# Moving the index score products of a two-block transformer kernel from the end of each projection tile to three places inside it

## Chip, cores and metric

The kernel runs on one core of a Trainium2 chip. The metric is device time in microseconds (us) of one execution; the median of three runs of the kernel before is 3087.84 us (3087.29 to 3089.44).

## What is computed

The reference is a stack of two kinds of transformer block over 512 tokens of width 1024. The first kind (latent attention, Fourier mixing and windowed attention, then a feed-forward and a gated embedding) is run twice, the second kind once. The change lies in the second kind, which begins with one wide projection `h @ w_in` and feeds, among others, a sparse attention. The keys of this attention are picked by an "index branch":

```python
logits = einsum('bqhd,bsd->bqhs', q_idx, k_idx) * IDX_DIM ** -0.5          # 8 heads of 64
score  = einsum('bqh,bqhs->bqs', w_idx * IDX_HEADS ** -0.5, relu(logits))
score  = where(admissible, score, -inf)
_, sel = top_k(score, 128)                                                 # per query
```

## The kernel before, in words

Weights arrive as a stream of units of 1 MB (128 partitions by 2048 columns, that is 16 blocks of 128x128). Every unit is split into a high part (`w_hi`, ScalarE, L923) and a low part (`w_lo`, VectorE, L1318), and every block of a projection is three TensorE matmuls of 512 columns: high by high, low by high, high by low (`mac`, L504 to L506). SyncE starts the load of a unit when VectorE has split the one that was in the same buffer before (`lo_ready`); there are two buffers of each kind.

The stage "z2" is the wide projection of the second block: 23 tiles (n = 0 to 22) of 8 blocks (j = 0 to 7), so 24 matmuls in a tile and two tiles in a unit. Results go round PSUM banks 0 to 3. `run` (L515) writes TensorE's order: for each tile it waits for a free bank, goes through the blocks, signals `tile_done`, and calls `after(n)`. Tiles 4 to 7 are the index queries `qi`, tile 8 the index keys `ki`, tile 9 holds the head weights.

Between these tiles the index branch is worked off: 32 score products, t = 0 to 31, one for each of 4 query blocks b = t // 8 and 8 heads hh = t % 8. A product (L823) is a float32 matmul with 64 rows of contraction and (b+1)*128 columns; its rows are partitions 0 to 63 for an even head and 64 to 127 for an odd one. It goes to one of two score banks, t % 2. `idx_items(n)` gives three products to each tile from n = 11 (two to n = 21). ScalarE takes the relu into `sq[:, t % 2]` (L1219), VectorE multiplies by the head's weight and adds to `score` (`add_idx`, L1723 and L1726). The rings are two deep:

```python
                    if t >= 2:
                        pe.wait_ge(idx_relu, t - 1)       # L820, TensorE: relu of product t-2
```

```python
                    if t >= 2:
                        act.wait_ge(idx_added, t - 1)     # L1217, ScalarE: add of product t-2
```

All three products of tile n stand behind its last block (`after_z2`, L816). ScalarE's and VectorE's orders are written by hand as well: each calls `evac_z2(n)` for both tiles of a unit, and then its part of the split of the unit two further on. Within `evac_z2(n)` the tile's own result comes first and the three relus or adds of that tile behind it. On ScalarE tile 14 also has four casts of `ua_hi` (L971) and a table load for the Gelu; on VectorE tiles 14 to 17 have the pooling windows (`pool`, L1704 to L1711), and tiles 18 to 22 end with one round of `take_top8` (L1740, L1741).

The stages behind z2 are "lru" (12 single blocks), the merges "bm2" and "am", and the sparse attention "dsa", in which two more blocks of a projection stand behind each step.

Of the kernel before, what the change touches and what calls it, by code (L numbers as in the profile page):

```python
# [11 lines left out]
ACT = mybir.ActivationFunctionType  # L12
AX_X = mybir.AxisListType.X

P = 128
S = 512
# [209 lines left out]
def block_kernel(nc, stream, xT, pT, memT, vec1, cst, pos, out):  # L226
    with ExitStack() as ctx:
# [16 lines left out]
        sq = sb("sq", 108, [2, S])  # L244
# [109 lines left out]
        SCORES, TURNED, VALUES = bank[4:6], bank[6], bank[7]  # L354
# [63 lines left out]
        idx_done = sem("idx_done")  # L418
        idx_relu = sem("idx_relu")
# [37 lines left out]
        def idx_items(n):  # L457
            return range(min(3 * max(n - IDX_FROM, 0), IDX_ITEMS), min(3 * max(n - IDX_FROM + 1, 0), IDX_ITEMS))
        assert idx_items(22).stop == IDX_ITEMS


        NORMS = {
# [32 lines left out]
        def _(pe):  # L495
# [15 lines left out]
                    pe.wait_ge(tile_free, c.at("T", st, n - 3))  # L511
                return bank[t % 4]

            def run(c, st, operand, first=0, last=None, width=S, after=None, together=False):


                tiles = TILES[st]
                u0 = c.base[st]["U"]
                ends = {}
                for n, t in enumerate(tiles):  # L520
                    for j, b in enumerate(t):
                        ends[b // BLK] = (n, j)
                seen = -1 if first == 0 else tiles[first - 1][-1] // BLK
                if together:
                    pe.wait_ge(lo_ready, c.at("U", st, 1))
                    seen, first = 0, 2
                    two = [free_bank(c, st, n)[:, 0:width] for n in range(2)]
                    for j in range(KD):
                        for n in range(2):
                            xh, xl, need = operand(n, j)  # L530
                            if need is not None:
                                pe.wait_ge(need[0], need[1])
                            mm = mac(two[n], u0 % 2, tiles[n][j], P, xh, xl, j == 0, j == KD - 1)
                            if j == KD - 1:
                                mm.then_inc(tile_done, 1)
                    if after is not None:
                        after(1)
                for n in range(first, len(tiles) if last is None else last):
                    t = tiles[n]
                    ps = free_bank(c, st, n)[:, 0:width]  # L540
                    for j, b in enumerate(t):
                        u = b // BLK
                        if u > seen:
                            pe.wait_ge(lo_ready, c.at("U", st, u + 1))
                            seen = u
                        xh, xl, need = operand(n, j)
                        if need is not None:
                            pe.wait_ge(need[0], need[1])
                        mm = mac(ps, (u0 + u) % 2, b % BLK, P, xh, xl, j == 0, j == len(t) - 1)
                        if j == len(t) - 1:  # L550
                            mm.then_inc(tile_done, 1)
                        elif ends[u] == (n, j):
                            mm.then_inc(part_done, 1)
                    if after is not None:
                        after(n)

# [253 lines left out]
            def after_z2(n):  # L810
                if n == 10:
                    pe.wait_ge(act_took, c.at("A", "z2", 9))
                    for t in range(ST):
                        mm = nc.tensor.transpose(TURNED[:, t * P:(t + 1) * P], vwT[:, t * P:(t + 1) * P], ident)
                    mm.then_inc(vw_turned, 1)
                for t in idx_items(n):  # L816
                    if t == 0:
                        pe.wait_ge(tile_free, c.at("T", "z2", 9))
                    if t >= 2:
                        pe.wait_ge(idx_relu, t - 1)  # L820
                    b, hh = t // 8, t % 8
                    r = slice(64 * (hh % 2), 64 * (hh % 2) + 64)
                    nc.tensor.matmul(SCORES[t % 2][:, 0:(b + 1) * P], qi[r, hh // 2, b * P:(b + 1) * P], ki[r, 0:(b + 1) * P],  # L823
                                     start=True, stop=True).then_inc(idx_done, 1)
            run(c, "z2", lambda n, j: (h_hi[:, j, :], h_lo[:, j, :], (res_split, c.at("R", "norm1", j + 1)) if n == 0 else None),
                together=True, after=after_z2)

            def lru_operand(n, j):
                if n < 4:
# [43 lines left out]
        for table, stages in ((RR1, STAGES1), (RR2, STAGES2)):  # L873
            n = 0
# [32 lines left out]
        def _(act):  # L907
# [287 lines left out]
            link(nc.scalar.activation(lruc[:, 2, 0:4], lruc[:, 1, 0:4], ACT.Ln, bias=1.0))  # L1195
            nc.scalar.activation(lruc[:, 3, 0:4], ap4, ACT.Relu, scale=-1.0).then_inc(softplus_ready, 1)

            def evac_z2(n):
                if n < 4:
                    take_hi(c, "z2", n, n, lx[:, n, :])  # L1200
                elif n < 8:
                    take_hi(c, "z2", n, n, qi[:, n - 4, :])
                elif n == 9:
                    take_hi(c, "z2", n, 8, vwT[:, :])
                elif 14 <= n < 18:
                    if n == 14:
                        for j in range(4):
                            split_hi(c, "z2", j, ua_hi[:, j, :], ua[:, j, :], (res_ready, result_value(c, "z2", j)))
                    take_hi(c, "z2", n, n - 5, lg[:, n - 14, :], ACT.Gelu_apprx_tanh)
                elif n == 19:  # L1210
                    for j in range(4):
                        r = c.base["z2"]["R"] + 4 + j
                        split_hi(c, "z2", 4 + j, pool_hi[:, j, :], res[:, r % 4, :], (res_ready, result_value(c, "z2", 4 + j)))
                for t in idx_items(n):
                    act.wait_ge(idx_done, t + 1)
                    if t >= 2:
                        act.wait_ge(idx_added, t - 1)  # L1217
                    w = (t // 8 + 1) * P
                    nc.scalar.activation(sq[:, t % 2, 0:w], SCORES[t % 2][:, 0:w], ACT.Relu).then_inc(idx_relu, 1)  # L1219
            stage_loop(c, "z2", evac_z2)  # L1220

            def evac_lru(n):
# [75 lines left out]
        def _(dve):  # L1298
# [416 lines left out]
            def add_idx(t):  # L1715

                b, hh = t // 8, t % 8
                w = (b + 1) * P
                dve.wait_ge(idx_relu, t + 1)
                if t == 0:  # L1720
                    dve.wait_ge(res_ready, result_value(c, "z2", 3))
                if hh == 0:
                    ins = nc.vector.tensor_scalar(score[:, b, 0:w], sq[:, t % 2, 0:w], wsc[:, b, hh:hh + 1], None, ALU.mult)  # L1723
                else:
                    dve.wait_ge(idx_added, t)
                    ins = nc.vector.scalar_tensor_tensor(out=score[:, b, 0:w], in0=sq[:, t % 2, 0:w], scalar=wsc[:, b, hh:hh + 1],  # L1726
                                                         in1=score[:, b, 0:w], op0=ALU.mult, op1=ALU.add)
                ins.then_inc(idx_added, 1)
# [16 lines left out]
            A_Z2 = {n: n for n in range(8)} | {9: 8} | {n: n - 5 for n in range(14, 18)}  # L1745

            def evac_z2(n):
                if n in A_Z2:
                    dve.wait_ge(act_took, c.at("A", "z2", A_Z2[n] + 1))
                    pass_on(c, "z2", n)  # L1750
                    if 4 <= n < 8:
                        conv(n - 4)
                    elif n >= 14:
                        if n == 14:
                            dve.wait_ge(tile_free, c.at("T", "z2", 14))
                        pool(n - 14)
                elif 10 <= n < 14:
                    if n == 10:
                        dve.wait_ge(pad_ready, 1)
                    copy_out(c, "z2", n, 0, pz[:, n - 10, PADW:PADW + S], lambda ps: ps[:, :], wait_act=False)  # L1760
                    if n == 10:
                        dve.wait_ge(vw_turned, 1)
                        link(nc.vector.tensor_copy(vw[:, :, :], TURNED[:, :].rearrange("p (t d) -> p t d", t=ST)))

                        link(nc.vector.tensor_scalar(wsc[:, :, :], vw[:, :, HD:HD + 8], 8 ** -0.5, None, ALU.mult))
                else:
                    dst = {8: ki, 22: kk}.get(n)
                    copy_out(c, "z2", n, 0, qd[:, n - 18, :] if dst is None else dst[:, :], lambda ps: ps[:, :], wait_act=False)
                for t in idx_items(n):
                    add_idx(t)  # L1770
                if n >= 18:
                    if n == 18:
                        dve.wait_ge(idx_added, 16)
                        hide(1)
                    take_top8(rounds[n - 18])
# [379 lines left out]
```

## Time and profile before

| what | value |
| --- | --- |
| runs | 3087.84 us median (3087.29 to 3089.44) |
| profiled execution | span of 3080.3 us from first to last instruction; the page gives no other time of it |
| TensorE matmuls busy | 2884.8 us, 94% of the span |
| VectorE busy | 1541.7 us, 50% |
| ScalarE busy | 1072.0 us, 35% |
| GpSimd busy | 458.7 us, 15% |
| granted TensorE clock | 0.969 of full speed over the span |
| the products, L823 | 64 matmuls, between 2126.7 and 2204.6 us |

Times in the rows are microseconds from the start of the span. The median of the runs is 7.5 us above the span. A matmul's own duration contains the passage through the array; the time that it costs is read from one start to the next. A row of the timeline may merge matmuls of one line ("x4").

### The profile page before, as it was taken

The numbers are of one execution on the slowest core, as the hardware profiler recorded it, in microseconds if no ns is written. First come the engines' busy times: TensorE is split into PE (matmuls) and PEld (weight loads), VectorE is DVE, ScalarE is ACT, GpSimd is POOL, SyncE is SP. The second block draws the span as 40 slices with busy tenths as digits, with TensorE's granted clock in tenths as the row PEclk, the third lists the DMA queues.
The fourth block names the chain that finished last, engine by engine and source line by source line (L and its number), as shares of the span: only waits on it lengthen the run. The fifth ranks groups of instructions, "written<-read, shape, count | busy, mean of one in ns | idle before, by whom it ended". The sixth has DMA issues, their size and how long they took to land. (4 is left out here: it accounts for less than half of the span.)

```text
span 3080.3 us, 34797 instructions
## 1 busy us (share of the span) xinstructions
PE 2884.8 (94%) x12356; PEld 2227.7 (72%) x12356; DVE 1541.7 (50%) x2229; ACT 1072.0 (35%) x1631; POOL 458.7 (15%) x283
## 2 busy tenths in 40 slices
PE   6998999899999899899989999989999998899997
PEld 4875567688887688546768888767676676578886
DVE  4356684534324534768444342454578735553333
ACT  4234433332323433443233222342533333432221
POOL 1010011311102301001131111230011113121101
PEclk9999999999999899999999999999998899999999
DMA  3221012222232222101222223222222122122232
GB/s 125 96 83 55 15 55 83 69 96 95 95 110 91 68 96 86 65 1 56 82 82 82 95 95 109 86 69 91 82 97 81 42 71 80 41 82 95 95 109 83
DMA packets 37047, 245.80 MB, mean 80 GB/s; under 512 B 4144, under 2 KB 5168, under 8 KB 7984
## 3 DMA queue, kind: packets, MB, share of 16 engines
q1 hardware_dynamic: 33600, 239.09, 22.8%
q10 hardware_dynamic: 3312, 4.93, 0.5%
q8 instruction: 82, 1.34, 0.2%
q14 instruction: 53, 0.43, 0.0%
HBM read 241.91 MB, written 2.10 MB: 79 GB/s over the span
## 5 line engine op out<-in xcount | busy, mean ns | idle before, releaser
L504 PE MATMUL bank<-h_hi,w_hi 128*128 128x512 f32 x2152 | 865.3, 402 | 53.8 <-DVE h_lo L1401 40.8
L505 PE MATMUL bank<-h_lo,w_hi 128*128 128x512 f32 x2152 | 846.1, 393 | 0.0
L506 PE MATMUL bank<-h_hi,w_lo 128*128 128x512 f32 x2152 | 845.9, 393 | 0.0
L1318 DVE TENSOR_TENSOR w_lo<-raw,w_hi 128x2048 fp32r<-128x2048 f32 x225 | 519.4, 2309 | 559.4 <-ACT w_hi L923 384.1
L504 PEld LDWEIGHTS bank<-h_hi,w_hi 128*128 128x128 f32 x2152 | 409.4, 190 | 161.7 <-issue 35.7
L505 PEld LDWEIGHTS bank<-h_lo,w_hi 128*128 128x128 f32 x2152 | 409.6, 190 | 86.8 <-issue 4.7
L506 PEld LDWEIGHTS bank<-h_hi,w_lo 128*128 128x128 f32 x2152 | 408.9, 190 | 87.1
L923 ACT ACTIVATE w_hi<-raw 128x2048 fp32r<-128x2048 f32 x137 | 261.9, 1911 | 313.5 <-PE bank L506 303.5
L504 PE MATMUL bank<-a_hi,w_hi 128*128 128x512 f32 x528 | 205.4, 389 | 0.0
L505 PE MATMUL bank<-a_lo,w_hi 128*128 128x512 f32 x528 | 205.4, 389 | 0.0
L506 PE MATMUL bank<-a_hi,w_lo 128*128 128x512 f32 x528 | 205.4, 389 | 0.0
L1873 POOL TENSOR_TENSOR a_lo<-res,a_hi 128x512 f32 x66 | 85.8, 1300 | 632.8 <-ACT a_hi L1061 632.8
L1508 DVE TENSOR_TENSOR res<-bank,rstd 128x512 f32<-128x512 f32 x66 | 45.6, 691 | 235.2 <-PE bank L506 235.2
L1891 POOL TENSOR_TENSOR w_hi<-raw,cst_sb 128x2048 fp32r<-128x2048 f32 x20 | 72.0, 3602 | 531.5 <-PE bank L506 490.3
L1061 ACT ACTIVATE a_hi<-res 128x512 f32 x66 | 41.7, 632 | 301.4 <-DVE res L1511 301.4
L1018 ACT ACTIVATE pT<-bank 128x512 f32<-128x512 f32 (+3 forms) x168 | 82.8, 493 | 150.7 <-PE bank L641 147.8
L1065 ACT ACTIVATE w_hi<-raw 128x2048 fp32r<-128x2048 f32 x66 | 125.5, 1902 | 0.0
L1897 POOL TENSOR_TENSOR x<-x,sg 128x512 f32<-128x512 f32 x60 | 108.9, 1820 | 95.1 <-DVE sg L1366 62.7
L504 PEld LDWEIGHTS bank<-a_hi,w_hi 128*128 128x128 f32 x528 | 99.1, 188 | 20.7
L506 PEld LDWEIGHTS bank<-a_hi,w_lo 128*128 128x128 f32 x528 | 99.1, 188 | 20.6
L505 PEld LDWEIGHTS bank<-a_lo,w_hi 128*128 128x128 f32 x528 | 99.1, 188 | 20.4
L932 ACT ACTIVATE sq<-bank 128x512 f32<-128x512 f32 x64 | 38.3, 598 | 211.6 <-PE bank L506 211.2
(351 smaller groups left out, 4030.5 us busy)
## 6 DMA issues: line engine op xcount, KB each, us to landing
raw<-in_stream SPq DMA_DIRECT2D x226, 1024.0 KB, 4.9
x<-in_xT SPq DMA_DIRECT2D x2, 1024.0 KB, 12.0
out_T<-x ACTq DMA_DIRECT2D x8, 256.0 KB, 2.1
p_f<-in_pT ACTq DMA_DIRECT2D x2, 512.0 KB, 3.7
memf<-in_memT ACTq DMA_DIRECT2D x1, 1024.0 KB, 5.6
cst_sb<-in_cst ACTq DMA_DIRECT2D x1, 411.5 KB, 6.2
pos_i<-in_pos ACTq DMA_DIRECT2D x1, 258.0 KB, 8.8
vec<-in_vec ACTq DMA_DIRECT2D x2, 26.0 KB, 1.7
```

The lines of the kernel that those rows point to most:

```text
L504: nc.tensor.matmul(ps, wh, xh, start=start, stop=False)
L505: nc.tensor.matmul(ps, wh, xl, start=False, stop=False)
L506: return nc.tensor.matmul(ps, wl, xh, start=False, stop=stop)
L923: nc.scalar.activation(w_hi[v % 2][:, :], raw[v % 2][:, :], ACT.Copy).then_inc(hi_ready, 1)
L1018: nc.scalar.activation(a["pT"][h % 2][:, 0:n, b * P:(b + 1) * P], TURNED[:, 0:n * P].rearrange("p (t q) -> p t q", t=n), ACT.Copy).then_in ...
L1061: nc.scalar.activation(a_hi[:, bass.ds(i * 2 + p, 1), :].rearrange("p a s -> p (a s)"), res[:, p, :], ACT.Copy).then_inc(res_hi, 1)
L1065: nc.scalar.activation(w_hi[v][:, :], raw[v][:, :], ACT.Copy).then_inc(hi_ready, 1)
L1318: nc.vector.tensor_tensor(w_lo[s][:, :], raw[s][:, :], w_hi[s][:, :].bitcast(F32), ALU.subtract).then_inc(lo_ready, 1)
L1508: nc.vector.tensor_tensor(res[:, p, :], bank[(t0 + 2 * p + 1) % 4][:, :], rstd[:, 0, :], ALU.mult).then_inc(tile_free, 1)
L1873: nc.gpsimd.tensor_tensor(a_lo[:, bass.ds(i * 2 + p, 1), :].rearrange("p a s -> p (a s)"), res[:, p, :], a_hi[:, bass.ds(i * 2 + p, 1), :] ...
L1891: nc.gpsimd.tensor_tensor(w_hi[v % 2][:, :], raw[v % 2][:, :], ones[:, 0:1].to_broadcast([P, UC]), ALU.mult).then_inc(pool_hi_ready, 1)
L1897: nc.gpsimd.tensor_tensor(x[:, m, :], x[:, m, :], sg[:, m % 2, :], ALU.add).then_inc(x_ready, 1)
```

## The change

The products of tile n are no longer all behind its last block: the first stands behind block j = 1, the second behind j = 4, the third behind j = 7. `run` gets a hook `within(n, j)` that is called behind each block. ScalarE and VectorE take the first two relus or adds of a tile ahead of the tile's own result, and the third behind it, as before. The waits themselves are unchanged, and so are the transposes behind tile 10.

```diff
+        IDX_AFTER = (1, 4, 7)
@@ run
-            def run(c, st, operand, first=0, last=None, width=S, after=None, together=False):
+            def run(c, st, operand, first=0, last=None, width=S, after=None, together=False, within=None):
@@
                         elif ends[u] == (n, j):
                             mm.then_inc(part_done, 1)
+                        if within is not None:
+                            within(n, j)
@@ TensorE, z2
-                for t in idx_items(n):
+
+            def logits_idx(n, j):
+
+                items = idx_items(n)
+                for t in items[IDX_AFTER.index(j):][:1] if j in IDX_AFTER else ():
                     if t == 0:
                         pe.wait_ge(tile_free, c.at("T", "z2", 9))
                     if t >= 2:
@@
-                together=True, after=after_z2)
+                together=True, after=after_z2, within=logits_idx)
@@ ScalarE
+            def relu_idx(t):
+                act.wait_ge(idx_done, t + 1)
+                if t >= 2:
+                    act.wait_ge(idx_added, t - 1)
+                w = (t // 8 + 1) * P
+                nc.scalar.activation(sq[:, t % 2, 0:w], SCORES[t % 2][:, 0:w], ACT.Relu).then_inc(idx_relu, 1)
+
             def evac_z2(n):
+                for t in idx_items(n)[0:2]:
+                    relu_idx(t)
...
-                for t in idx_items(n):
-                    act.wait_ge(idx_done, t + 1)
-                    if t >= 2:
-                        act.wait_ge(idx_added, t - 1)
-                    w = (t // 8 + 1) * P
-                    nc.scalar.activation(sq[:, t % 2, 0:w], SCORES[t % 2][:, 0:w], ACT.Relu).then_inc(idx_relu, 1)
+                for t in idx_items(n)[2:]:
+                    relu_idx(t)
@@ VectorE
             def evac_z2(n):
+                for t in idx_items(n)[0:2]:
+                    add_idx(t)
...
-                for t in idx_items(n):
+                for t in idx_items(n)[2:]:
                     add_idx(t)
```

## Rows read from the trace of the kernel before

**Rows 1.** Busy time, clock and DMA share in the stretch with the products.
```profile
core 0: us, PE busy (x) PEld busy (x) DVE busy (x) ACT busy (x) POOL busy (x), PEclk, DMA share, GB/s
2126.00:2206.00 80.00, 75.22 (x315) 52.14 (x314) 47.65 (x72) 30.06 (x51) 12.21 (x8) 1.00 0.20 66
```

**Rows 2.** TensorE's waits in the same stage: engine, line, releaser, us, times, longest.
```profile
PE bank L823 <- ACT sq L1219: 4.8, 10, 0.7
```

**Rows 3.** TensorE's timeline, undisturbed blocks of tile 7, 18 matmuls apart.
```profile
start us, us, engine line op out<-in xcount [idle before <-releaser]
2100.02 0.39 PE L506 MATMUL bank<-h_hi,w_lo 128*128 128x512 f32 x1
...
2104.10 0.39 PE L506 MATMUL bank<-h_hi,w_lo 128*128 128x512 f32 x1
```

**Rows 4.** TensorE's timeline, first matmul of tile 11.
```profile
2121.00 0.48 PE L504 MATMUL bank<-h_hi,w_hi 128*128 128x512 f32 x1
```

**Rows 5.** TensorE's timeline, end of tile 20, its products, first matmul of tile 21.
```profile
2194.50 0.39 PE L506 MATMUL bank<-h_hi,w_lo 128*128 128x512 f32 x1
2194.82 1.13 PE L823 MATMUL bank<-ki,qi 64*128 64x512 f32 x4
2196.63 1.12 PE L823 MATMUL bank<-ki,qi 64*128 64x512 f32 x2 [0.68 <-ACT sq L1219]
2197.68 0.50 PE L504 MATMUL bank<-h_hi,w_hi 128*128 128x512 f32 x1
```

**Rows 6.** TensorE's timeline, the two products of tile 21, start of tile 22.
```profile
2203.35 1.13 PE L823 MATMUL bank<-ki,qi 64*128 64x512 f32 x4
2204.41 0.50 PE L504 MATMUL bank<-h_hi,w_hi 128*128 128x512 f32 x1
2204.74 0.39 PE L505 MATMUL bank<-h_lo,w_hi 128*128 128x512 f32 x1
```

**Rows 7.** TensorE's timeline, third product of tiles 12, 14 and 17, next block.
```profile
2134.47 0.48 PE L823 MATMUL bank<-ki,qi 64*128 64x128 f32 x2 [0.36 <-ACT sq L1219]
2134.89 0.50 PE L504 MATMUL bank<-h_hi,w_hi 128*128 128x512 f32 x1
...
2148.89 0.70 PE L823 MATMUL bank<-ki,qi 64*128 64x256 f32 x2 [0.47 <-ACT sq L1219]
2149.51 0.50 PE L504 MATMUL bank<-h_hi,w_hi 128*128 128x512 f32 x1
...
2171.80 0.91 PE L823 MATMUL bank<-ki,qi 64*128 64x384 f32 x2 [0.57 <-ACT sq L1219]
2172.64 0.50 PE L504 MATMUL bank<-h_hi,w_hi 128*128 128x512 f32 x1
```

**Rows 8.** TensorE's timeline, windowed attention: one 64-row product between two blocks.
```profile
348.96 0.40 PE L506 MATMUL bank<-h_hi,w_lo 128*128 128x512 f32 x1
349.29 0.91 PE L631 MATMUL bank<-kdup,qc 64*128 64x384 f32 x2
350.13 0.50 PE L504 MATMUL bank<-h_hi,w_hi 128*128 128x512 f32 x1
350.47 0.40 PE L505 MATMUL bank<-h_lo,w_hi 128*128 128x512 f32 x1
```

**Rows 9.** TensorE's timeline, latent attention: one 96-row product between two blocks.
```profile
248.72 0.39 PE L506 MATMUL bank<-h_hi,w_lo 128*128 128x512 f32 x1
248.95 1.02 PE L631 MATMUL bank<-k_a,q_a 96*128 96x512 f32 x2
249.41 0.80 PE L504 MATMUL bank<-h_hi,w_hi 128*128 128x512 f32 x1
250.04 0.40 PE L505 MATMUL bank<-h_lo,w_hi 128*128 128x512 f32 x1
```

**Rows 10.** ScalarE's timeline, tile 14: the casts and the table load.
```profile
2144.24 2.18 ACT L971 ACTIVATE ua_hi<-ua 128x512 fp32r<-128x512 f32 x4
2146.44 1.28 ACT L932 ACT_TABLE_LOAD   x1
```

**Rows 11.** VectorE in stage bm2; TensorE at the start of the sparse attention.
```profile
2239.97 0.69 DVE L1422 TENSOR_TENSOR merged<-bank,sg 128x512 f32<-128x512 f32 x1 [11.69 <-ACT sg L932]
...
2366.30 0.79 PE L631 MATMUL bank<-kk,qd 64*128 64x128 f32 x2 [5.77 <-DVE rstd L1425]
```

## The prediction

> **What bounds the kernel now.** I read the stretch with the products first. TensorE is busy for 75.22 of 80 us at the full clock, VectorE for 47.65, ScalarE for 30.06, and the DMA engines for a fifth [rows 1]. So TensorE sets the pace here, and only what TensorE issues or waits for can change the time. Next its waits: all that is named is ten waits of a product for a relu, 4.8 us together [rows 2]. They are what the change can remove: the third product of a tile needs the bank of the first, and so the relu of a product issued just before it. Tile 21 has two products and no wait, which makes ten waits in the eleven tiles.
>
> Then the price of all 32 products. Undisturbed, 18 steps from one matmul to the next take 2104.10 - 2100.02 = 4.08 us, 0.2267 us each [rows 3], so a tile of 24 matmuls takes 5.44 us. From the first matmul of tile 11 (2121.00) [rows 4] to the first of tile 22 (2204.41) [rows 6] there are 83.41 us. Eleven tiles take 59.85 of them; the products with their waits cost **23.56 us**.
>
> **What makes them cheap is the pair.** The first two products of a tile stand together, and one uses partitions 0 to 63, the other 64 to 127. Four matmuls (two products) of 512 columns show 1.13 us, and two matmuls (one product) show 1.12 [rows 5]. From the start of a pair to the next block it is 2204.41 - 2203.35 = 1.06 us [rows 6]; from the start of a single product it is 2197.68 - 2196.63 = 1.05 us [rows 5]. The second product of a pair is free. The change takes every pair apart.
>
> **The change part by part.** (1) It adds no instruction, moves no DMA, and does not change what has to be computed. (2) It puts each of the 32 products by itself between two blocks. What one costs there: the step from the last block to the product is 2194.82 - 2194.50 = 0.32 us [rows 5], the product to the next block is 0.42, 0.62, 0.84 us at 128, 256, 384 columns [rows 7] and 1.05 at 512, and the first step within the block after is 2204.74 - 2204.41 = 0.33 [rows 6]. Without the product the first and the last of these would be two ordinary steps, 0.454 us. So it costs 0.62, 0.82, 1.04 and 1.25 us at the four widths, 3.73 for one of each. The single products of rows 5 and 7 stand behind a wait, which might flatter them. The windowed attention has the very thing, one 64-row product of 384 columns between two blocks with no wait: 350.47 - 348.96 = 1.51 us, less 0.454 is 1.06 [rows 8], against my 1.04. With eight products of each width the sum is 8 x 3.73 = 29.8 us.
>
> (3) The steps behind a break are a little slow. Tile 21 takes 2203.35 - 2197.68 = 5.67 us from its first matmul to its pair [rows 5, 6]; less 0.33 and 0.32 that leaves 5.02 for 22 steps, 0.2282 each, 0.033 us more per tile than at 0.2267. The 23.56 us hold one such tail per tile, and three breaks per tile may make up to three. If every tail stays whole that is 32 x 0.033 = 1.1 us, if they cost nothing more 0; I take 0.8, since the nine steps between two breaks hold most of a tail. The products then cost 29.8 + 0.8 = 30.6 us.
>
> (4) The ten waits go; they are inside the 23.56. The difference is 30.6 - 23.56 = **+7.0 us**. As a cross-check by tile: tile 21 now pays 2 x 1.25 = 2.50 us where it paid 1.06 + 0.32 + 0.33 - 0.454 = 1.26, so +1.24. Tile 20 paid the 0.32, then 1.81 from pair to third product and 1.05 onward, and the 0.33: 3.06 in all; it now pays 3.75, +0.69, though a wait is gone. In the wait of about 0.7 us TensorE already covered most of what a separate product costs.
>
> (5) Moved on ScalarE: two relus of each tile now stand ahead of its eviction and wait for products behind blocks 1 and 4. Behind them on this engine is only the eviction of the same tile, not ready before block 7. Tile 14 is the tight place: `ua_hi` casts (2.18 us) and table load (1.28 us) [rows 10] now begin after the relu behind block 4, some 5.4 us into a tile that takes 5.44 + 3 x 0.82 = 7.9 us. Eviction and third relu follow, done about 9.9 us in. Product 13, which needs this relu, stands behind block 4 of tile 15, at 7.9 + 15 x 0.2267 + 0.82 = 12.1 us. Margin 2 us, so I cost it at nothing; if that cover were gone, TensorE would wait.
>
> (6) Moved on VectorE: two adds go ahead of the tile's own work, where it now waits for a relu in the middle of the tile. Behind that wait is only the copy of the same tile; the bank it frees is needed four tiles later. The low split of a unit still follows the odd tile at once, and the SyncE load that it releases is for a buffer used two units on; with the queues a fifth busy [rows 1] nothing waits for it. The pooling of tiles 14 to 17 delays the third add, and with it a relu one product later, but every relu has at least three blocks and a product (over 2.6 us) more than before. Costed at nothing.
>
> The sum in microseconds is the same against the span (3080.3) or the median of the runs (3087.84), which stands 7.5 us above it: 3087.84 + 7.0 = **3094.8 us**. A difference of 0.2% (6.2 us) is about what a measurement of this kernel can tell from no change, so my forecast stands just over that line.
>
> **Bounds.** What one product costs between blocks has a far lower end: the latent attention has a 96-row product of 512 columns between blocks, and 250.04 - 248.72 = 1.32 us less 0.454 is 0.87 [rows 9], 0.38 under my 1.25. With 96 rows no pair is possible, and the step into it is 0.23 and not 0.32. Were the 32 products as smooth, they would cost 30.6 - 32 x 0.38 = 18.4 us, and the change would give -5.2 us. Rows 8 have the very shape, so I take 1.25. The upper end is rows 8's extra 0.02 on each, +0.6 us.
>
> **The rivals.** A, faster: a product's weights are loaded beneath the block before it, so that a product is all streaming, as in rows 9; it decides if the extra per product is under (23.56 - 18.4) / 32 = 0.16 us of the 0.38. Then 3087.84 - 5.2 - 1 (the tails gone too) = 3081.7 us. For it: a weight load of an ordinary block is hidden in this way at every step of 0.2267 us. Against it: rows 8.
>
> The Trainium skill, "TensorE: Matmul & The Clock Gate", section "Step-by-step: what each phase is for", says that a weight load is pulled ahead of running matmuls when the row groups do not conflict or it goes to the background buffer. By the second half of that rule A would hold, with 3081.7 us; rows 8 and 5 speak against it, since a 64-row product costs more than its stream there.
>
> B, slower still: a new wait takes the place of the old one, in tiles 14 to 18, where ScalarE's or VectorE's moved work makes a relu late and a product stands in the middle of an open tile. At 1 us in each of four or five tiles that is +4.5, so 3099 us. For it: in the kernel before, relus there wait for adds behind the pooling. Against it: the margins of (5) and (6).
>
> C, no change: a later stage gives the time back. The sparse attention starts with TensorE waiting 5.77 us for VectorE [rows 11]. If VectorE got there by its own backlog, a slower z2 would shrink that wait, to 3087.84 + 7.0 - 5.8 = 3089.0 us. Against it: in bm2 VectorE idles 11.69 us for a ScalarE result [rows 11], which follows TensorE's tiles, so the backlog does not reach back to z2.
>
> **How the numbers follow.** My forecast has 0.78, with its own range 3092 to 3097. Rows 8's price and full tails would give +7.9, no tails and the low roundings +6.1: I put 0.50 above the line of 6.2 us and 0.28 under. A has 0.06 (0.04 faster, 0.02 within), B 0.08 (slower), C 0.08 (within). Faster 0.04, within 0.38, slower 0.58. The range takes in C and most of B: 3089 to 3099.
>
> **What would show it.** Right: no row of L823 with x4 and no pair starting within 0.1 us; no wait of L823 for `sq`; a product to the next block at 0.42, 0.62, 0.84 and 1.05 us; first matmul of tile 11 to first of tile 22 about 83.4 + 7.0 = 90.4 us; the stages behind z2 shifted by that and no more. Wrong: a product at under 0.9 us in all at 512 columns (A); waits of L823 in tiles 14 to 18 (B); a stretch of z2 that is 7 us longer with a span that is not (C).

## The result, and the profile after

The changed kernel takes 3093.66 us, the median of 13 runs (3088.89 to 3095.1), against 3087.84 us for 13 runs of the kernel before. The ratio is 1.0018 with a 95% interval of 1.001 to 1.0026: slower by 3 to 8 us. Forecast were 3094.8 us and a range of 3089 to 3099. The two profiled executions differ by 6.8 us in span (3080.3 and 3087.1).

The busy times of the stage come first (columns as in rows 1).

```profile
core 0: us, PE busy (x) PEld busy (x) DVE busy (x) ACT busy (x) POOL busy (x), PEclk, DMA share, GB/s
2126.00:2206.00 80.00, 80.00 (x289) 49.33 (x287) 45.23 (x68) 28.95 (x47) 11.01 (x8) 1.00 0.19 66
```

TensorE now shows busy for all of the 80 us, against 75.22 in [rows 1]. Yet it starts 289 matmuls in them, and 315 before. The busy share rose and the work done fell. The 4.8 us that were idle before are the ten waits of [rows 2]. All other time shows as busy in both kernels, whether blocks follow at their 0.23 us or a product stands between them, because the row of a matmul (0.39 us for one of a block) lasts past the start of the next.

The view of TensorE's waits over 2117 to 2222 us has no row for a product any more, where [rows 2] had ten. The view of the product's line (L830 in the changed kernel) says what its two queues waited for.

```profile
L830 PEld LDWEIGHTS bank<-ki,qi x64: 182/184/186, 2122.5 to 2208.6; 64*128 64x128 f32 x64
L830 PE MATMUL bank<-ki,qi x64: 272/481/693, 2122.5 to 2209.1; 64*128 64x128 f32 x16, 64*128 64x256 f32 x16, 64*128 64x384 f32 x16, 64*128 64x512 f32 x16
its engine sat idle before it (us, times) until:
  issue: 11.5, 32
```

Each of the 32 products now has its own gap ahead of its weight load (PEld, the queue of weight loads), 0.36 us on average, and none waits for the relu. The same 64 matmuls have the same durations as before. Only their company has changed.

TensorE's timeline, the first and second products of tile 20 and the blocks round them:

```profile
2195.92 1.12 PE L830 MATMUL bank<-ki,qi 64*128 64x512 f32 x2
2196.97 0.50 PE L505 MATMUL bank<-h_hi,w_hi 128*128 128x512 f32 x1
2197.30 0.39 PE L506 MATMUL bank<-h_lo,w_hi 128*128 128x512 f32 x1
...
2198.92 0.39 PE L507 MATMUL bank<-h_hi,w_lo 128*128 128x512 f32 x1
2199.24 1.12 PE L830 MATMUL bank<-ki,qi 64*128 64x512 f32 x2
2200.29 0.50 PE L505 MATMUL bank<-h_hi,w_hi 128*128 128x512 f32 x1
2200.62 0.39 PE L506 MATMUL bank<-h_lo,w_hi 128*128 128x512 f32 x1
```

The steps are 0.32, 1.05 and 0.33 us, those of [rows 5, 6]; at the other widths 0.41, 0.63 and 0.84 us stand in the place of the 1.05, as in [rows 7]. In the kernel before, the row of the pair had "x4" and 1.13 us for twice the work.

The stretch from the first matmul of tile 11 to the first of tile 22:

```profile
2120.98 0.48 PE L505 MATMUL bank<-h_hi,w_hi 128*128 128x512 f32 x1
...
2211.76 0.39 PE L505 MATMUL bank<-h_hi,w_hi 128*128 128x512 f32 x1
```

It is 90.78 us, where it was 83.41 [rows 4, 6]: +7.37 us. Less the 59.85 us of the eleven tiles without products, the 32 products cost 30.9 us instead of 23.6. Behind z2 two rows answer to [rows 11]; the first is VectorE's, the second TensorE's.

```profile
2247.15 0.69 DVE L1434 TENSOR_TENSOR merged<-bank,sg 128x512 f32<-128x512 f32 x1 [11.68 <-ACT sg L939]
...
2373.45 0.79 PE L634 MATMUL bank<-kk,qd 64*128 64x128 f32 x2 [5.76 <-DVE rstd L1437]
```

They start 7.18 and 7.15 us later, after the same idle times (11.69 and 5.77 before). The stages between pass the delay on unchanged, up to 0.2 us. From the end of the stretch to the end of the span it is 875.9 us before and 875.3 after, so in these two executions at most 0.6 us are given back.

### The profile page after: what moved, and what is told of

It reads as the page before. It is cut to its first block and busy times, and to the rows that moved or that the text cites. A ratio compares the mean times of both kernels' runs of the same rounds, so it can differ in the third digit from the quotient of the medians.

```text
span 3087.1 us, 34795 instructions
## 1 busy us (share of the span) xinstructions
PE 2897.7 (94%) x12356; PEld 2229.8 (72%) x12356; DVE 1540.4 (50%) x2229; ACT 1073.2 (35%) x1631; POOL 457.3 (15%) x283
```

## The experiments

In each trace I read the stretch from tile 11 to tile 22, because the profiled executions already differ by up to 6 us ahead of it (tile 11 starts between 2120.98 and 2126.91), where the kernels are the same. Each interval of a ratio is about 5 to 8 us wide, so the runs give the sign and rough size, and the stretch tells kernels apart. Times are against runs of the kernel before on the same chip.

**The new order on ScalarE and VectorE alone.** From the changed kernel:

```diff
-        IDX_AFTER = (1, 4, 7)
+        IDX_AFTER = (7,)
@@ logits_idx
-                for t in items[IDX_AFTER.index(j):][:1] if j in IDX_AFTER else ():
+                for t in items if j == 7 else ():
```

> The new order on ScalarE and VectorE alone; TensorE's three products stand behind the last block of a tile, as before. 'Stretch' is the time from the first matmul of tile 11 to the first of tile 22: 83.4 us before, 90.8 after. Theory (the pairs taken apart on TensorE are the whole cost): stretch 83 to 84 us, ten waits of L830 for sq of about 4.8 us in total, time as before within 0.5 us. Rival (the new order on the other two engines costs): stretch over 86 us, with waits of L830 longer than 1 us.

Measured: 3087.11 us against 3088.62, ratio 0.9994 (0.9985 to 1.0004). Its stretch goes from 2125.57 to 2209.24, 83.67 us. The waits of TensorE in the stage, and tile 15's products in its timeline:

```profile
PE bank L830 <- ACT sq L1210: 4.8, 10, 0.7
```

```profile
2159.77 0.70 PE L830 MATMUL bank<-ki,qi 64*128 64x256 f32 x4
2160.94 0.70 PE L830 MATMUL bank<-ki,qi 64*128 64x256 f32 x2 [0.47 <-ACT sq L1210]
2161.57 0.50 PE L505 MATMUL bank<-h_hi,w_hi 128*128 128x512 f32 x1
```

The ten waits of [rows 2] are back with the pairs, and the loss is gone. The order of the relus and adds costs nothing that can be seen (0.26 us of stretch). The cost of the change is on TensorE. The expectation of a time within 0.5 us can't be checked: the runs give 1.5 us less, with an interval of -4.6 to +1.2.

**Pairs kept, waits gone.** The pair behind block 1, the third product behind block 5; all relus and adds of a tile ahead of its own result:

```diff
-        IDX_AFTER = (1, 4, 7)
+        IDX_AFTER = {1: slice(0, 2), 5: slice(2, 3)}
@@ logits_idx
-                for t in items[IDX_AFTER.index(j):][:1] if j in IDX_AFTER else ():
+                for t in items[IDX_AFTER[j]] if j in IDX_AFTER else ():
@@ evac_z2 of ScalarE and VectorE
-                for t in idx_items(n)[0:2]:
+                for t in idx_items(n):
...
-                for t in idx_items(n)[2:]:
```

> The first two products of a tile stand together behind block 1, the third behind block 5: pairs kept, waits gone. Theory: 21 breaks in place of 32, priced by their widest product at 0.62, 0.82, 1.04 and 1.25 us, 19.7 us and 0.5 for tails: stretch 80.1 us, 3.3 less than before and 10.7 less than after. Rival (what costs is that a product stands inside an open tile, whatever it is): per tile two breaks inside a tile in place of one outside, stretch over 84 us.

Measured: 3083.2 us against 3088.62, ratio 0.9983 (0.9974 to 0.9992). Stretch 80.52 us, 0.4 more than expected. TensorE's timeline, the third product of tile 20 and the pair of tile 21:

```profile
2196.54 1.12 PE L830 MATMUL bank<-ki,qi 64*128 64x512 f32 x2
2197.59 0.50 PE L505 MATMUL bank<-h_hi,w_hi 128*128 128x512 f32 x1
...
2200.55 1.13 PE L830 MATMUL bank<-ki,qi 64*128 64x512 f32 x4
2201.61 0.50 PE L505 MATMUL bank<-h_hi,w_hi 128*128 128x512 f32 x1
```

1.05 us for one product, 1.06 for two, both inside an open tile and without a wait. So it does not matter that a tile is open. With the pairs left whole, being rid of the 4.8 us of waits is worth 2.9 us net, since the third product still pays its own break.

**All products in pairs.** Sixteen places, 5.5 blocks apart:

```diff
-        IDX_AFTER = (1, 4, 7)
+        IDX_AT = [89 + 11 * p // 2 for p in range(IDX_ITEMS // 2)]
+
+        def idx_pairs(n, js=range(8)):
+            return [t for p, g in enumerate(IDX_AT) if g // 8 == n and g % 8 in js for t in (2 * p, 2 * p + 1)]
...
```

The lines left out make all three engines take the products of a tile from `idx_pairs`. ScalarE and VectorE take a pair ahead of the tile's own result, or behind it if the pair stands behind block 7.

> All 32 products in 16 pairs, one every 5.5 blocks. Theory: four breaks of each width, 4 x 3.73 = 14.9 us and 0.4 to 0.5 for tails: stretch 75.2 us, time 8.2 us less than before (-0.27%). Rival (the price belongs to the product, not to the break): 32 products cost as in after, stretch about 90 us, or, with a relu not ready at the next pair, waits of L83x for sq and a stretch over 78.

Measured: 3079.42 us against 3088.62, ratio 0.9969 (0.9957 to 0.9982). Stretch 75.58 us, and no wait for `sq`. Two pairs from TensorE's timeline, at 256 and 384 columns:

```profile
2159.53 0.70 PE L832 MATMUL bank<-ki,qi 64*128 64x256 f32 x4
2160.16 0.50 PE L508 MATMUL bank<-h_hi,w_hi 128*128 128x512 f32 x1
...
2164.48 0.92 PE L832 MATMUL bank<-ki,qi 64*128 64x384 f32 x4
2165.32 0.50 PE L508 MATMUL bank<-h_hi,w_hi 128*128 128x512 f32 x1
```

0.63 and 0.84 us, what a single product of the width costs. The 32 products cost 75.58 - 59.85 = 15.7 us, half of the 30.9 of the changed kernel. The price goes by the break, and the second product in it is free.

**Single products over all 128 rows.** A product sums two heads here, so the logits of the index branch are other ones.

```diff
-                    r = slice(64 * (hh % 2), 64 * (hh % 2) + 64)
+                    r = slice(0, P)
```

> As after, but each product is taken over all 128 partitions, so that it sums two heads: the logits of the index branch are those of two heads added, and the rest is unchanged. Theory (0.38 us of every single product is the change between 64 and 128 rows of the array, not the stream): 0.24, 0.44, 0.66 and 0.87 us a product as in rows 9, 17.7 us in all: stretch 77.6 to 78.6 us, about 5 us less than before and 12 less than after. Rival (the extra belongs to a float32 matmul among the rounded ones, or to the smaller weight load): stretch as in after, 90.8 us.

Measured: 3082.87 us against 3088.62, ratio 0.9983 (0.9973 to 0.9992). Stretch 2121.25 to 2199.59, 78.34 us. TensorE's timeline, one product of 512 columns:

```profile
2188.30 0.39 PE L507 MATMUL bank<-h_hi,w_lo 128*128 128x512 f32 x1
2188.53 1.02 PE L830 MATMUL bank<-ki,qi 128*128 128x512 f32 x2
2188.98 0.80 PE L505 MATMUL bank<-h_hi,w_hi 128*128 128x512 f32 x1
2189.62 0.40 PE L506 MATMUL bank<-h_lo,w_hi 128*128 128x512 f32 x1
```

The weight loads of this product, and those of the 64-row product that starts at 2199.24 in the changed kernel:

```profile
2188.30 0.41 PEld L830 LDWEIGHTS bank<-ki,qi 128*128 128x128 f32 x2
```

```profile
2199.23 0.29 PEld L830 LDWEIGHTS bank<-ki,qi 64*128 64x128 f32 x2 [0.35 <-issue]
```

The 128-row load begins together with the last matmul of the block before, 0.23 us ahead of its product. The 64-row load begins 0.31 us after the last matmul of its block (2198.92), 0.01 us ahead of its product. So 128-row weights are loaded beneath the block, and 64-row weights are not.

From block to block 2189.62 - 2188.30 = 1.32 us, the same as in [rows 9], and 0.38 less than 0.32 + 1.05 + 0.33 for 64 rows. Type, width, place and number are those of the changed kernel; only the rows differ, and with them the size of the weight load. So it is not the float32 type that costs. That it is not the small load by itself either is shown by the groups of four below, which have the same 64 small loads. And 96 rows are as smooth as 128 [rows 9]. In this stretch the step between 64-row and 128-row matmuls costs 90.78 - 78.34 = 12.4 us, or 0.39 us for each product's way in and out.

The Trainium skill, "TensorE: Matmul & The Clock Gate", section "The mechanism", finds weight loads overlapping running matmuls only where the row groups differ. A 64-row product between 128-row blocks shares rows with both, and by that rule its load is exposed, as here. But a 128-row product shares them too, and its load is hidden (2188.30 above), so the rule as it stands does not tell the two apart and does not give the 0.39 us. What in the engine holds the 64-row load back no run here shows.

**Groups of four.** Eight places, ten blocks apart, and four score banks:

```diff
-        IDX_AFTER = (1, 4, 7)
+        IDX_AT = [97 + 10 * q for q in range(IDX_ITEMS // 4)]
+        SCORES4 = (bank[4], bank[5], bank[6], bank[7])
@@ logits_idx
-                    if t >= 2:
-                        pe.wait_ge(idx_relu, t - 1)
+                    if t >= 4:
+                        pe.wait_ge(idx_relu, t - 3)
...
```

The lines left out write product t to `SCORES4[t % 4]`, let ScalarE read it there, and let all three engines take the products of a tile in groups of four.

> The 32 products in eight groups of four, one every ten blocks from block 1 of tile 12, over four score banks: two pairs share one way in and one way out. Theory: a break has 0.38 us for its way in and out and the stream 0.24, 0.44, 0.66, 0.87 for each pair; eight breaks are 8 x 0.38 + 4 x 2.21 = 11.9 us and 0.2 for tails: stretch 72.0 us, 3.6 less than with sixteen pairs. Rival 1 (the price is per pair, not per break): stretch 75.6 as with sixteen pairs. Rival 2 (ScalarE or VectorE fall behind with four relus and adds at once): waits of TensorE for sq of over 1 us in tiles 14 to 18.

Measured: 3077.28 us against 3088.23, ratio 0.9969 (0.9957 to 0.998). Stretch 2126.23 to 2198.23, 72.00 us. TensorE's timeline, one group of 512 columns:

```profile
2190.42 0.39 PE L511 MATMUL bank<-h_hi,w_lo 128*128 128x512 f32 x1
2190.74 1.99 PE L833 MATMUL bank<-ki,qi 64*128 64x512 f32 x8
2192.66 0.50 PE L509 MATMUL bank<-h_hi,w_hi 128*128 128x512 f32 x1
2192.99 0.40 PE L510 MATMUL bank<-h_lo,w_hi 128*128 128x512 f32 x1
```

1.92 us from the group to the next block, against 1.06 for one pair: the second pair adds 0.86 us, its stream alone. The way in and out is paid once per group. Four products take two streams, not four and not one: the even and the odd head of a pair, in different halves of the rows, run together, and the next pair follows. No run puts two products of the same half side by side, so that the halves are the reason is a reading. ScalarE and VectorE keep up, with no wait of TensorE for `sq`. By the stretch this is the best of the kernels tried, 11.4 us shorter than before; the runs can't separate it from the sixteen pairs.

**The changed kernel again.**

> The changed kernel once more, beside runs of the kernel before of the same hour: the stretch should be 90.8 us again and the time 7 us more than before (+0.23%) if all that the stretch adds reaches the end; rival: about 5.6 us (+0.18%), so that 1 to 2 us are given back behind it.

Measured: 3093.23 us against 3088.23, ratio 1.0018 (1.0009 to 1.0027), and a stretch of 90.79 us. The ratio is the same as the first time, and its interval (2.8 to 8.3 us) holds both 7 and 5.6 us, so the runs did not tell the two apart. The trace speaks against the rival: from the end of the stretch to the end of the span it is 875.1 us, against 875.9 before, so 0.8 us are given back and not 1 to 2.

## Why the prediction was right

By its own steps:

- **What bounds.** TensorE's order alone sets the stage. The order of the other two engines on its own moved the stretch by 0.26 us.
- **The pair is free.** Shown: 1.05 us for one and 1.06 for two, in the same kernel; the same at 256 and 384 columns; half the price when all products are in pairs.
- **Step 2, the price of a single product.** 29.8 us for 32, from steps that came out the same to 0.01 us. Averaged over the eight products of each width, the prices in the changed kernel are 0.62, 0.83, 1.04 and 1.26 us, 30.0 in all. The row of another stage with the very shape [rows 8] was a better guide than the smooth one [rows 9], as chosen.
- **Step 3, the tails.** I took 0.8 us, and 30.9 - 30.0 = 0.9 is left for them. The 0.2 us of step 2 and the 0.1 here are most of the difference between +7.0 and the +7.37 of the stretch.
- **Step 4, the waits.** They went, all ten, and were worth less than what took their place.
- **Step 5, ScalarE in tile 14.** Shown below. Tile 14 starts at 2143.33, and the third relu ends at 2153.18, 9.85 us in (9.9 predicted). Product 13, which needs it, starts at 2155.82, 2.6 us later. The margin held.

```profile
2148.82 2.18 ACT L978 ACTIVATE ua_hi<-ua 128x512 fp32r<-128x512 f32 x4
2151.02 1.28 ACT L939 ACT_TABLE_LOAD   x1
2152.31 0.60 ACT L939 ACTIVATE lg<-bank 128x512 f32<-128x512 f32 x1
2152.80 0.38 ACT L1210 ACTIVATE sq<-bank 128x256 f32<-128x256 f32 x1
```

- **Rival A** (a product is all streaming) is what the 128-row experiment shows: its weights are loaded beneath the block, and the stretch is 78.34 us, 5.1 less than before, where the rival's price said 5.2. It takes 128 rows, which this change does not have.
- **Rival B** (a new wait) did not come: no wait of a product in any tile.
- **Rival C** (given back by the sparse attention's wait) did not come either: that wait is 5.76 us, 7.15 of the 7.37 us arrive there, and 6.8 us are left at the end of the span.

The mechanism stands by the stretch. In the time as run, +7.0 was forecast and the ratio gives +5.6 us. That is under the line of 6.2 us (0.2%) above which the prediction put a chance of 0.50, while the stretch, at +7.4, is above it. The runs could tell the change from none all the same, with an interval of 3.1 to 8.0 us. The median lies 1.1 us under the forecast although the stretch grew by 0.4 more than forecast, so part of that agreement is luck.

What stays open is this difference between runs and stretch. The interval holds both, and the other kernels fall on either side of their stretch: by their ratios -5.2 us for -2.9 with pair and single, -9.6 for -7.8 with sixteen pairs, -9.6 for -11.4 with groups of four. The granted clock of the runs points the same way. The 11 executions of the second run of the changed kernel have a mean of 0.9682, the 17 of the kernel before beside them 0.9668. Groups of four, the only kernel that gained less than its stretch, is the only one with a lower clock (0.9660) than the kernel before beside it. Why the clock differs was not tried.

## What to carry to other kernels

Before removing a wait that the profile names, price what its removal takes apart. Here ten waits of 0.25 to 0.68 us stood in a layout in which products went out two for the price of one, and spreading the products to be rid of the waits cost more than the waits. Before moving small matmuls apart, price the way in and out of their row shape (start to start, from the last large matmul before to the second one after), and count breaks, not matmuls. To remove such a wait, keep the group whole and move it as one, or make it larger with more score banks.

## What was not expected of the hardware

The sparse attention starts at a granted clock of 0.50, the 1.2 GHz level. In the kernel before it is still 1.00 from 2362 to 2364 us, while TensorE waits for VectorE, and falls in the last 2.3 us of this wait of 5.8 us. How long it stays there differs between executions of one kernel. The rows have the columns of rows 1. The first is of the kernel before, the second of the profiled execution after, the third of the changed kernel run again, all from 2.1 to 2.5 us before the stage's first product.

```profile
2364.00:2405.00 41.00, 36.73 (x115) 25.16 (x116) 28.41 (x62) 16.35 (x41) 11.13 (x9) 0.50 0.10 30
```

```profile
2371.00:2412.00 41.00, 36.59 (x114) 25.01 (x115) 28.56 (x62) 16.50 (x41) 11.27 (x9) 0.50 0.10 30
```

```profile
2375.00:2416.00 41.00, 35.36 (x126) 24.36 (x127) 27.50 (x62) 16.21 (x40) 10.93 (x8) 0.59 0.13 43
```

And here is the kernel with a pair and a single product, from 1.2 us before that product:

```profile
2368.00:2409.00 41.00, 36.18 (x155) 25.16 (x156) 30.55 (x71) 17.96 (x47) 10.03 (x7) 0.71 0.16 52
```

At a mean of 0.50, 0.59 and 0.71 of the clock, 114, 126 and 155 matmuls are done in 41 us. Not all of this lasts. From the first product of the stage to its last it is 99.2 us before, 99.0 after, 98.7 in the second run and 95.9 with pair and single, so the last one won 3.3 us here in its profiled execution. Whether that is chance or hangs on when the stage begins was not tried. It is nearly half of the effect studied, and so the verdicts here rest on the stretch in the trace, and on the runs for their sign.
